# Main RMSNorm issued inside the pre-GLA phase, constant set-up issued next to the first norm

## The reference, cut to what matters

```
h    = rmsnorm(x, norm_w)                        # 1024 + 128 rows of x per core ("main")
proj = h @ w_in                                  # a_u a_v a_g b_q b_k b_v b_r b_g x_q x_g
log_a = log_sigmoid(b_r @ b_wa + b_ba) / 16      # gates of the GLA
o_b, s = gla(b_q, b_k, b_v, log_a, s0)           # sequential over the tokens of a prompt
branches = [a_o * silu(a_g), o_b * silu(b_g), o_x * silu(x_g)]
y = rmsnorm(x + branches @ w_out)
```

## Time and profile before

| | |
|---|---|
| median of 6 runs | 1148.78 us (1146.08 to 1149.95) |
| the profiled execution | 1144.06 us, span of its slowest core 1142.5 us |
| spans of the 8 cores in it | 1121.9 to 1142.5 us, granted clock 0.845 to 0.855 |
| busy on the slowest core | PE 70%, PE weight load 39%, DVE 32%, ACT 23%, POOL 11% |

### The profile page before, as it was taken

One profiled execution on the slowest core, in us unless ns is written; L12 is line 12 of the kernel. 1 busy time (PEld: TensorE's weight loads), 2 busy tenths in 40 slices (PEclk: granted clock), 3 DMA queues, 4 the chain that ended last, 5 costly groups with the idle time before them and its releaser, 6 DMA issues.

```text
span 1142.5 us, 14090 instructions; the slowest of 8 cores (1121.9 to 1142.5 us)
## 1 busy us (share of the span) xinstructions
PE 795.7 (70%) x4734; PEld 440.4 (39%) x4734; DVE 366.9 (32%) x672; ACT 262.8 (23%) x554; POOL 127.2 (11%) x146
## 2 busy tenths in 40 slices
PE   0459595645996877736655787999954338999882
PEld 0324263534444544433332453444521334444331
DVE  0526232217344544523120143211035312123223
ACT  0623134024332322233230222011131001111101
POOL 2510000115000102011112000000100330000000
PEclk9988798765798998957778798999985557999997
DMA  3753421684307356440303997332530794232342
GB/s 60 249 58 48 63 38 74 96 205 182 56 2 110 54 127 129 119 72 6 56 1 55 164 166 111 56 56 38 62 50 0 102 129 65 74 124 106 139 148 110
DMA packets 95913, 101.64 MB, mean 89 GB/s; under 512 B 12881, under 2 KB 90722, under 8 KB 90978
## 3 DMA queue, kind: packets, MB, share of 16 engines
q0 software_dynamic: 68560, 48.89, 31.1%
q1 hardware_dynamic: 26642, 51.84, 14.2%
q10 hardware_dynamic: 640, 0.01, 0.0%
HBM read 133.72 MB, written 15.89 MB: 131 GB/s over the span
## 4 chain that ended last, share of the span: by engine, by line
PE 50%; DMA 18%; DVE 12%; ACT 8%; issue 7%; POOL 3%; SPq 2%; DVEq 0%; ACTq 0%; POOLq 0%
PE P L303 27%; PE P L297 8%; PE P L1128 5%; DMA ckb_142<-ck 4%; DMA wsl_20<-w_in 3%; DMA xsl_149<-xp 3%; DVE rinv L1023 2%; SPq L100 1%; PE P L825 1%; DMA xsl_78<-xp 1%; DMA xsl_32<-xpre 1%; PE P L438 1%; DVE hT L348 1%; DMA wsl_21<-w_in 1%; DVE Sst L577 1%
## 5 line engine op out<-in xcount | busy, mean ns | idle before, releaser
L303 PE MATMUL P<-hT,wsl_21 128*128 128x512 bf16 (+3 forms) x944 | 182.1, 357 | 3.8 <-DVE branchT L390 1.8
L303 PE MATMUL P<-hT,wsl_20 128*128 128x512 bf16 (+5 forms) x896 | 161.9, 342 | 22.7 <-DMA wsl_20<-w_in 16.7
L1128 PE MATMUL P<-wout,branchT 128*128 128x512 bf16 x576 | 128.2, 385 | 8.6 <-DVE ysl_150 L1131 6.3
L303 PEld LDWEIGHTS P<-hT,wsl_21 128*128 128x128 bf16 (+1 forms) x944 | 94.8, 114 | 92.4 <-issue 28.9
L303 PEld LDWEIGHTS P<-hT,wsl_20 128*128 128x128 bf16 (+2 forms) x896 | 81.6, 106 | 100.6 <-issue 38.8
L297 PE MATMUL P<-wsl_20,hT 128*128 128x384 bf16 x416 | 79.3, 348 | 29.5 <-DMA wsl_20<-w_in 16.1
L1128 PEld LDWEIGHTS P<-wout,branchT 128*128 128x128 bf16 x576 | 56.6, 99 | 80.0 <-issue 15.2
L297 PE MATMUL P<-wsl_21,hT 128*128 128x384 bf16 x416 | 73.4, 331 | 4.0 <-DVE branchT L390 2.3
L297 PEld LDWEIGHTS P<-wsl_20,hT 128*128 128x128 bf16 x416 | 42.5, 103 | 59.5 <-issue 37.6
L297 PEld LDWEIGHTS P<-wsl_21,hT 128*128 128x128 bf16 x416 | 40.5, 99 | 29.5 <-issue 6.5
L348 DVE TENSOR_TENSOR hT<-T,normw_col 128x1024 bf16<-128x1024 bf16 x34 | 41.6, 1225 | 11.4 <-PE T L341 9.6
(11 more groups left out here) (322 smaller groups left out, 941.1 us busy)
## 6 DMA issues: line engine op xcount, KB each, us to landing
wsl_21<-w_in POOLq DMA_DIRECT2D x8, 1536.0 KB, 12.5
wsl_20<-w_in POOLq DMA_DIRECT2D x7, 1536.0 KB, 13.6
wout<-w_out POOLq DMA_DIRECT2D x4, 2048.0 KB, 47.6
xsl_149<-xp SPq DMA_DIRECT2D x8, 1024.0 KB, 7.4
yp<-ysl_150 SPq DMA_DIRECT2D x4, 1024.0 KB, 4.7
yp<-ysl_151 SPq DMA_DIRECT2D x4, 1024.0 KB, 5.4
xsl_32<-xpre SPq DMA_DIRECT2D x2, 1024.0 KB, 7.2
xsl_33<-xpre SPq DMA_DIRECT2D x2, 1024.0 KB, 8.7
```

The lines of the kernel that those rows point to most:

```text
L303: K.op("pe", lambda e, k=k: e.matmul(ps[0:M, 0:ntok], lhsT=wslot[:, k, c0:c0 + M], rhs=hT[:, k, tok0:tok0 + ntok], start=(k == 0), stop=(k ...
L1128: K.op("pe", lambda e, k=k, q=q, pi=pi: e.matmul(P[pi][:, 0:512], lhsT=branchT[:, k, t * 128:(t + 1) * 128], rhs=wout[:, k, q * 512:(q + 1 ...
```

## The change

The constant set-up moves, as a block and unchanged, to the place directly ahead of the pre norm, and its closing barrier is dropped: the first norm is issued behind it with nothing between. The norm's code becomes a generator (`norm_gen`) that yields after each tile, with the number of slots taken from its buffers; without a junk buffer the Square writes its unused output into the tile's own bf16 slot. The pre norm now writes `branchT`, which is not otherwise in use yet, so that `hT` is free, and the main norm is built as a generator `side` with three load slots and two bf16 slots, which the pre GLA steps between its own generators. The separate main norm ahead of the main GLA is gone.

```diff
-        with ExitStack() as cs:
-            Wf = sb(cs, "Wf", [128, 4, 128], F32)
...
-            K.barrier()
-        def norm_T(stack_bufs, src_list, dstT, dstk, wcol, wcolk):
+        def norm_gen(stack_bufs, src_list, dstT, dstk, wcol, wcolk):
             xsl, xsb_, jnk = stack_bufs
+            nx, nbf = len(xsl), len(xsb_)
...
+                jo, jk = (jnk[:], "jnk") if jnk is not None else (xsb_[sq_][:], bk)
+                K.op("act", lambda e: e.activation(out=jo, in_=xsl[sx][:], func=AF.Square, accum_out=st[s][:, 0:1]),
+                     reads=[xk], writes=[jk, sk])
...
-            for i in range(min(3, n)):
+            for i in range(min(nx - 1, n)):
                 load(i)
             front(0)
             transposes(0)
+            yield
             for i in range(n):
                 if i + 1 < n:
                     front(i + 1)
                 back(i)
-                if i + 3 < n:
-                    load(i + 3)
+                if i + nx - 1 < n:
+                    load(i + nx - 1)
                 if i + 1 < n:
                     transposes(i + 1)
+                yield
...
-                    run1((qk_gen("q" if with_out else "k", w1slot, w1k), 4), (gg, 1))
+                    if side is not None:
+                        run1((qk_gen("q" if with_out else "k", w1slot, w1k), 4), (gg, 1), (side, 1))
+                    else:
+                        run1((qk_gen("q" if with_out else "k", w1slot, w1k), 4), (gg, 1))
                     wdone()
                     wprefetch()
...
-                            run((stage1(hp, wslot, wk, True), 1))
+                            if side is not None:
+                                run((stage1(hp, wslot, wk, True), 2), (side, 1))
+                            else:
+                                run((stage1(hp, wslot, wk, True), 1))
...
-            norm_scope([(dr["xpre"], 8, 0)], normw_col, "normw_col", hT, "hT")
+            with ExitStack() as cs:
+                Wf = sb(cs, "Wf", [128, 4, 128], F32)
...
+                norm_scope([(dr["xpre"], 8, 0)], normw_col, "normw_col", branchT, "hTp")
...
-            gla_phase(hT, "hT", NPRE, [("p", t * 128) for t in range(8)], with_out=False)
+            with ExitStack() as sn:
+                xsl_s = [sb(sn, f"xsl{i}", [128, D], F32) for i in range(3)]
+                xsb_s = [sb(sn, f"xsb{i}", [128, D], BF16) for i in range(2)]
+                side = norm_gen((xsl_s, xsb_s, None), [(dr["xp"], 8, 0), (dr["xs"], 1, 1024)], hT, "hT", normw_col, "normw_col")
+                gla_phase(branchT, "hTp", NPRE, [("p", t * 128) for t in range(8)], with_out=False, side=side)
+                for _ in side:
+                    pass
+                K.barrier()
...
-            norm_scope([(dr["xp"], 8, 0), (dr["xs"], 1, 1024)], normw_col, "normw_col", hT, "hT")
```

More of the change, by code:

```diff
@@ L255, in build_program @@
-        if stop == 'consts':
-            K.barrier()
-            return nc
         jobs = []
@@ L324, in load @@
                 src, t, c0 = tl[i]
-                K.dma("sp", xsl[i % 4][:], src[t * 128:(t + 1) * 128, :], writes=[f"xsl{i % 4}"])
+                K.dma("sp", xsl[i % nx][:], src[t * 128:(t + 1) * 128, :], writes=[f"xsl{i % nx}"])
             def front(i):
-                s, sx, sq_ = i % 2, i % 4, i % 3
+                s, sx, sq_ = i % 2, i % nx, i % nbf
                 xk, bk, sk = f"xsl{sx}", f"xsb{sq_}", f"st{s}"
-                K.op("act", lambda e: e.activation(out=jnk[:], in_=xsl[sx][:], func=AF.Square, accum_out=st[s][:, 0:1]),
-                     reads=[xk], writes=["jnk", sk])
+                jo, jk = (jnk[:], "jnk") if jnk is not None else (xsb_[sq_][:], bk)
+                K.op("act", lambda e: e.activation(out=jo, in_=xsl[sx][:], func=AF.Square, accum_out=st[s][:, 0:1]),
+                     reads=[xk], writes=[jk, sk])
                 rstd_from_ss(st[s], sk, 1, float(D))
@@ L337, in transposes @@
             def transposes(i):
-                sq_ = i % 3
+                sq_ = i % nbf
                 for k in range(16):
@@ L396, in gate_feat, with gla_phase @@
                     yield
-        def gla_phase(hT, hTk, NT, tiles, with_out):
+        def gla_phase(hT, hTk, NT, tiles, with_out, side=None):
             blocks = []
@@ L794, in norm_scope @@
                     jnk = sb(ns, "jnk", [128, D], BF16)
-                    norm_T((xsl, xsb_, jnk), src_list, dstT, dstk, wcol, wcolk)
+                    for _ in norm_gen((xsl, xsb_, jnk), src_list, dstT, dstk, wcol, wcolk):
+                        pass
                     K.barrier()
-            norm_scope([(dr["xpre"], 8, 0)], normw_col, "normw_col", hT, "hT")
+            with ExitStack() as cs:
+                Wf = sb(cs, "Wf", [128, 4, 128], F32)
+                Wsf = sb(cs, "Wsf", [128, 4, 128], F32)
+                Wmb = sb(cs, "Wmb", [128, 4, 128], BF16)
+                Wsmb = sb(cs, "Wsmb", [128, 4, 128], BF16)
+                K.op("pool", lambda e: e.memset(Wsf[:], 0.0), writes=["Wsf"])
+                ck = dict(semkey="const")
+                K.dma("sp", normw_col[:], dr["norm_w"].rearrange("o (k p) -> p (o k)", p=128), writes=["normw_col"],
+                      allow_slow_non_contiguous=True, **ck)
+                K.dma("sp", memw_col[:], dr["mem_norm_w"].rearrange("o (k p) -> p (o k)", p=128), writes=["memw_col"],
+                      allow_slow_non_contiguous=True, **ck)
+                if stop == 'c2':
+                    K.barrier()
+                    return nc
+                K.dma("sp", wo_b[:], dr["b_onorm_w"].partition_broadcast(128), writes=["wo_b"], **ck)
+                K.dma("sp", abT[:], dr["a_bs"].rearrange("h i -> i h"), writes=["abT"], allow_slow_non_contiguous=True, **ck)
+                K.dma("sp", bwa[0:16, :], dr["b_wa"], writes=["bwa"], **ck)
+                K.dma("sp", bwa[16:17, :], dr["b_ba"], writes=["bwa"], part=True, **ck)
+                if stop == 'c3':
+                    K.barrier()
+                    return nc
+                K.dma("sp", Wf[:], dr["a_ws"].rearrange("h i j -> i h j"), writes=["Wf"], **ck)
+                for s in range(16):
+                    K.dma(["sp", "act"][s % 2], abTs[8 * s:8 * s + 8, :], dr["a_bs"][:, 0:8].rearrange("h i -> i h"), writes=["abTs"],
+                          part=(s > 0), allow_slow_non_contiguous=True, **ck)
+                    K.dma(["act", "sp"][s % 2], Wsf[8 * s:8 * s + 8, :, 8 * s:8 * s + 8], dr["a_ws"][:, 0:8, 0:8].rearrange("h i j -> i h j"),
+                          writes=["Wsf"], part=(s > 0), **ck)
+                if stop == 'c4':
+                    K.barrier()
+                    return nc
+                K.seal("const")
+                for src, srck, dst, dstk in ((Wf, "Wf", Wmb, "Wmb"), (Wsf, "Wsf", Wsmb, "Wsmb")):
+                    K.op("pool", lambda e, src=src: e.affine_select(out=src[:], in_=src[:], pattern=[[0, 4], [-1, 128]],
+                                                                    compare_op=ALU.is_ge, fill=0.0, base=0, channel_multiplier=1),
+                         reads=[srck], writes=[srck])
+                    K.op("pool", lambda e, src=src, dst=dst: e.tensor_copy(out=dst[:], in_=src[:]), reads=[srck], writes=[dstk])
+                if stop == 'c5':
+                    K.barrier()
+                    return nc
+                for src, srck, dst, dstk, tb in ((Wmb, "Wmb", WT, "WT", 0), (Wsmb, "Wsmb", WTs, "WTs", 1)):
+                    for h in range(4):
+                        K.op("pe", lambda e, src=src, h=h, tb=tb: e.transpose(out=T[tb][:, h * 128:(h + 1) * 128], in_=src[:, h, :],
+                                                                             identity=ident[:]),
+                             reads=[srck, "ident"], writes=[TK[tb]], signal=(h == 3))
+                    K.op("dve", lambda e, dst=dst, tb=tb: e.tensor_copy(out=dst[:].rearrange("p h i -> p (h i)"), in_=T[tb][:, 0:512]),
+                         reads=[TK[tb]], writes=[dstk])
+                norm_scope([(dr["xpre"], 8, 0)], normw_col, "normw_col", branchT, "hTp")
```

## The result

The changed kernel takes 1155.34 us (median, 1150.86 to 1165.1) against 1147.03 us for the kernel before in the same comparison: a ratio of 1.0084 with a 95% interval of 1.0052 to 1.0117. By that ratio it is slower by 9.6 us (6.0 to 13.4); the medians lie 8.3 apart. 1156.6 was predicted. Its profiled execution took 1156.92 us (core 7, span 1155.4).

What follows compares the result with a forecast made beforehand. The bound was taken to be a chain of waits through stages between barriers, leaving PE for DMAs at their joints. Terms −6.3 + 4 + 10.1 + 41.5 − 41.5 = +7.8 on 1148.78 gave 1156.6 us, range 1146 to 1167.

Steps and rivals of the forecast that it cites:

- Constants: Kernel start: without the barrier the pre norm's first load goes out earlier, at 16.05; −6.3 us, bounds −6.3 and −4.3.
- Main loads beside the gate weights: Start of the pre GLA: two 1 MB loads on SP delay BR, which PE waits for; +4 us, between 0 and 6.2.
- Tile 0 ahead of K1: Before K1, block 1's key matmuls: PE must first transpose main tile 0; +10.1 us, bounds 8.8 and 11.5.
- The drain: ACT's table loads before K1: by the skill page about 1.38 us extra each, sum about 2.8 higher; not counted.
- Tiles 1 to 8 and the value weights: K1's end to value matmuls: tiles at 3.55 us each, then both weight loads in 22.0; 54.9 against 13.4, +41.5.
- The old stage: Ahead of the main GLA: the separate main norm's stage is gone and gates start at once; −41.5 us, bounds −40.5 and −42.1.
- dearer by DMA: Rival: BR held back 6.2, tiles at 4.0, value-weight pair 25.2; +16 us, 1165; chance 0.18.
- The pair is quick: Rival: both value-weight loads land in 13.9 to 16.3 us; 1148.5 to 1151, no change; chance 0.15.
- It weaves: Rival: `side` spread over K0, K1 and value matmuls; −27 us, 1122; chance 0.12, shared with several terms at lower ends.

Runs made afterwards that it cites:

- e1: Kernel before with only the constant set-up moved next to the pre norm without its barrier, main norm still its own stage: 1133.58 against 1145.05 us, ratio 0.9919.
- e9: Changed kernel with only the third main load held until the gate and key weights have landed: ratio 1.0063 against before.
- e3: Changed kernel with the first three main loads held until BR and BK have landed: 1145.41 us, ratio 1.0011 against before.
- e8: Changed kernel, main norm woven into the value matmuls, first loads early behind gate and key weights, `back` before the next tile's `front`: 1107.05 against 1147.52 us, ratio 0.9648.

## Why the prediction came out right

The direction was right, and so was the mechanism of every term but one: one load more stood beside the gate weights than was counted. Sizes are means over the cores, after less before, from the table, where no core is named; the forecast was read from core 5.

- *Constants*: forecast −6.3, measured −7.6. SP's issues ran on as thought (the load at 15.19). On core 5 it left at 16.09, where 16.05 was forecast; over all cores it leaves 7.5 earlier on the mean. e1 has this half alone.
- *Main loads beside the gate weights*: forecast +4 with an upper bound of 6.2, measured +8.1, past that bound. The failed step is "SP now issues two 1 MB loads". The generator's `load(2)` stands behind tile 0's `back` in the code, but its slot is free from the start, and on SP's queue nothing stands between. The third went out at once, at 55.15, within BR's own issue (55.03 to 56.39). e9 puts two loads at 4.4 (10.7 − 6.3), e3 none at −0.1.
- *Tile 0 ahead of K1*: forecast +10.1, measured +10.4. The row of engines was as forecast, with one table load in it (110.68) and a PE idle of 8.89 ended by POOL's scaling.
- *The drain*: the prediction left open whether a table load on a busy ACT costs more than the load, as the Trainium skill, page "ScalarE: Activation LUTs", section "What ACT_TABLE_LOAD costs", states. Here ACT was busy until 110.42 + 0.19 = 110.61, the load began at 110.68 and Sqrt at 111.97. No drain of 1.38 shows, and the trace disagrees with the page.
- *Tiles 1 to 8 and the value weights*: forecast 54.9 from K1's end to the values and +41.5; measured 57.1 and +44.3, within the bounds. The pace was 3.6 to 3.7 on every core (3.63 on core 7) against 3.55; in the working of that pace 2.0 + 0.7 + 2.0 + 2.0 is 6.7 and not 6.8, which moves nothing. The pair took 23.5 on the mean against 22.0. On core 5 it was 22.7, and its bytes flowed at 171 GB/s, near the 165 of the earlier trace rows that the forecast kept for both loads. On core 7 they flowed at 150, and its 25.5 lies a little past the upper bound of 25.2. So two such loads do not always get less than one; why the cores differ stays open. By the Trainium skill, page "DMA: Bandwidth & Descriptors", section "Anatomy of one DMA — SWDGE (gpsimd) path", the pair would have been an estimated 16.4; the mean is 7 away, on the other side of my own value.
- *The old stage*: forecast −41.5, measured −41.0 (96.4 to 55.6, and 0.2 on the queries).

Their sum is +14.5 with the value stage's +0.3, where +7.8 was forecast and +4 to +12 was the forecast's own range. Of the 6.7 too much, 4.1 are BR's term and 2.8 the tiles' and the pair's. On core 5 alone the queries start 10.0 later. The timed difference is +9.6. The two profiled executions lie 4.6 us further apart than the medians, and one execution of each can't tell how much of the +14.5 is the kernel's own. The direction and the paths were foreseen; that 1155.34 lies within 1.3 of 1156.6 is in part luck, with a load uncounted.

Of the rivals, *dearer by DMA* is nearer to the stages' sum (+16 against +14.5), but not for its reasons: its 6.2 for BR lacks the third load, its 25.2 for the pair is reached on cores 1 and 7 alone, its 4.0 a tile on no core, and its 1165 is above the time. *The pair is quick* is out: no core took less than 21.4. *It weaves* is out as well, since no transposes stand among the changed kernel's value matmuls; e8, which does weave and also holds its loads behind the gate weights, is 40 us faster than before, more than the 27 that this rival gave.

## What to carry to other kernels

A piece of work that is moved to fill gaps brings its whole queue along: write down for each engine and each DMA queue what now stands in front of the next thing that PE waits for, loads and slots that are free early among them. Interleave a step in the order in which its pieces come free (transposes, then the reader of their bank, then the next tile's start), and issue its loads behind the small transfer that is waited for and ahead of the large ones. When a change of two parts loses a little, run each part alone first: here one was worth 0.8% and hid what the other cost.

## What the runs showed that I had not expected

- On core 7 a 64 KB load by POOL's queue lands after 6.4 to 6.9 us with no main load beside it, 11.0 beside two 1 MB loads of SP's queue (e9) and 14.7 beside three. Over all cores it is 3.9 to 6.9, 7.8 to 11.4 and, in the changed kernel, 11.7 to 14.7.
- Tile 0's scaling on POOL took 2.74 where DVE ran two f32 subtractions of 96x512 (0.69 and 0.68) beside it, and 1.97 for each of the eight later ones.
- Sixteen transposes took 1.86 in the stretch granted 0.53 and 0.95 between value matmuls at 0.96: a filler costs half in a stage that already holds the higher level, 2.4 GHz, after PE has been busy.
